# Two sparse-attention stages: VectorE divides both halves of a unit one behind the other, then masks both halves of the next unit

## The chip, the cores and the metric

The kernel runs on one core of a Trainium2 chip. The metric is the device time of one execution in microseconds (us), less is better. All operands are 32-bit floats; the large products are split into high and low parts by the kernel itself.

## What is computed

The reference is three transformer layers over 512 tokens of width 1024. The first two are an MLA (latent attention) layer and an HGRN2 layer, each with an MLP. The third mixes three branches of one input: a sparse attention with an index (DSA, 16 heads of 64, top 128 keys), a native sparse attention (NSA, 16 heads in 2 groups, with a compressed, a selected and a window part) and a state-space branch. The change touches the parts of DSA and NSA that are plain masked attention over 512 keys:

```python
# DSA, per block of 128 queries
s = jnp.einsum('bqhd,bqkd->bqhk', qb, k_sel).astype(jnp.float32) * scale
s = jnp.where((sel <= t[None, :, None])[:, :, None, :], s, NEG)
p = jax.nn.softmax(s, axis=-1).astype(v.dtype)
return jnp.einsum('bqhk,bqkd->bqhd', p, v_sel)
# NSA adds its parts, each times a gate
return gb[..., 0:1] * o_cmp + gb[..., 1:2] * o_slc + gb[..., 2:3] * o_win
```

The kernel does not gather the selected keys. It takes the scores of all keys up to the query's block and adds a mask that holds minus 1e30 where a key is not selected.

## The kernel before

The program is one stream of instructions for each engine, and the engines meet through semaphores alone. Its stages follow each other: MLA, MLP, HGRN, MLP, DSA, NSA, state space, output, MLP. The projections between are dense matmuls of TensorE (lines 385 to 387).

`Pairs` (line 1933) is the helper of the two stages that the change touches. A pair is two heads, one on partitions 0 to 63 and one on 64 to 127 of the same tile; these are its two halves. DSA has 8 pairs and one kind of key, so 8 units. NSA has 8 pairs and two kinds (selected keys and window keys, with their own masks), so 16 units. A unit n is worked in this way, and each step has a name that the text uses:

- **scores** (TensorE, line 2011): 16 matmuls of both halves, key times query, into PSUM banks that all units share. It waits until both halves of unit n-1 are masked, since it overwrites their scores.
- **mask** (VectorE, lines 2118 to 2129), one half: a copy of the query factors (2118), a zeroed sum (2121), four fused operations that scale the scores, add the mask and take the row's maximum (2124, of 128 x 128, 256, 384 and 512), and the maximum times minus one (2129). It waits for the scores of the unit.
- **exp** (ScalarE, line 2076), one half: four activations that also sum their rows. It waits for the mask of that half.
- **divide** (VectorE, lines 2136 to 2144), one half: one over the sum (2136), in NSA times the gate (2139), and four products that scale the probabilities (2144). It waits for the exp of that half.
- **turn** (TensorE, line 2028), one half: ten transposes in three pieces, into two PSUM banks in turn. The third piece waits until the first has been copied out.
- **keep** (ScalarE, line 2083), one half: three copies of the turned pieces out of PSUM.
- **out** (TensorE, line 2047): 16 matmuls of both halves, value times probabilities. In NSA, at each pair's first kind, 8 small products of the compressed part go in front (line 2690).
- **finish** (ScalarE, line 2090): the copy of a pair's result out of PSUM; each unit has one in DSA, every second in NSA.

GpSimd copies the pair's queries into place (line 1973). Every engine has a written order of its own, a `body` per turn of the loop. For one unit n they are, before the change:

- TensorE: turn(n, 0), out(n-1), turn(n, 1), scores(n+2)
- ScalarE: keep(n, 0), exp(n+1, 0), keep(n, 1), finish(n-1), exp(n+1, 1)
- VectorE: divide(n, 0), mask(n+1, 0), divide(n, 1), mask(n+1, 1)

The body of VectorE is the part that changes:

```python
for n in range(per):
    for half in range(2):
        divide(i, n, half)
        if n + 1 < per or nxt:
            mask(i, n + 1, half)
```

`per` is the number of units in a turn, 4 in both stages. DSA has two turns, both written out. NSA has four, the middle two in a loop of the engine. `nxt` is false only in the last turn, so that the last unit has divides and no masks.

Of the kernel before, what the change touches and what calls it, by code (L numbers as in the profile page):

```python
# [1932 lines left out]
class Pairs:  # L1933
# [178 lines left out]
    def dve(self, dve, M, gate=None):  # L2112
        A, V, per = self.name, self.view, len(self.items)

        def mask(i, n, half):
            u, kind = self.item(n)
            m, x = self.kinds[kind][2](half), 2 * (n % 2) + half
            dve.tensor_copy(V.inv[:, x, :], self.factors(M, i, u + n // per * self.unroll, half))
            dve.drain()
            dve.wait_ge(M.sem(f"{A}_scores"), i * per + (n + 1))  # L2120
            dve.memset(V.sum[:, x, :], 0.0)
            for t in range(QT):
                at = PAIR_S_AT[half][t]
                dve.tensor_tensor_reduce(V.p[x][:, CAUSAL_AT[t]:CAUSAL_AT[t] + S_LEN[t]], M.ps[:, at:at + S_LEN[t]],  # L2124
                                         m[:, CAUSAL_AT[t]:CAUSAL_AT[t] + S_LEN[t]],
                                         V.inv[:, x, t:t + 1], -3.0e38,
                                         ALU.add, ALU.max, V.top[:, x, t:t + 1])
            dve.drain()
            dve.tensor_scalar(V.ntop[:, x, :], V.top[:, x, :], -1.0, None, ALU.mult)\  # L2129
               .then_inc(M.sem(f"{A}_masked"), 1)  # L2130

        def divide(i, n, half):
            u, kind = self.item(n)
            x = 2 * (n % 2) + half
            dve.wait_ge(M.sem(f"{A}_exp"), i * (2 * per) + (2 * n + half + 1))
            dve.reciprocal(V.inv[:, x, :], V.sum[:, x, :])
            dve.drain()
            if gate:
                dve.tensor_tensor(V.inv[:, x, :], V.inv[:, x, :], gate(i, u + n // per * self.unroll, half, kind),
                                  ALU.mult)  # L2140
                dve.drain()
            for t in range(QT):
                s = V.p[x][:, CAUSAL_AT[t]:CAUSAL_AT[t] + S_LEN[t]]
                d = dve.tensor_scalar(s, s, V.inv[:, x, t:t + 1], None, ALU.mult)  # L2144
            d.then_inc(M.sem(f"{A}_probs"), 1)

        def body(i, nxt):
            for n in range(per):
                for half in range(2):
                    divide(i, n, half)  # L2150
                    if n + 1 < per or nxt:
                        mask(i, n + 1, half)

        mask(0, 0, 0)
        mask(0, 0, 1)
        self.loop(dve, body)


# [1698 lines left out]
```

## Time and profile before

| | us |
|---|---|
| median of 3 runs | 2777.93 |
| lowest, highest | 2777.47, 2778.92 |
| the profiled execution, its own time | 2784.97 |
| its span in the trace | 2783.2 |
| DSA's units, scores(0) to the next stage's first matmul | 1398.79 to 1486.27 |
| NSA's units, the same | 1652.35 to 1812.26 |

TensorE is busy for 95% of the span, VectorE for 59%, ScalarE for 41%. In the two stages named all three are busy for most of the time. A busy share is read with its stretch; the order in which the engines release each other is read from the timeline, where each row has a start, a duration, the engine, the line, the tiles written and read, and in brackets how long the engine was idle before it and what ended that. "issue" there means that the profile shows no releaser.

### The profile page before, as it was taken

What the parts mean: (1) busy time and instruction counts of PE and PEld (TensorE: products, weight loads), DVE (VectorE), ACT (ScalarE), POOL (GpSimd) and SP (SyncE); (2) the same over time, 40 slices, a digit from 0 to 9 for tenths busy, and PEclk for the clock granted to TensorE, in tenths of its full rate; (3) what the DMA queues carried; (4) which work ended last, traced back from release to release, by engine and by line L of the source; (5) the groups of instructions that cost most, each with busy time, mean ns of one, the idle gap of its engine ahead of it and who ended that gap; (6) DMA issues with size and microseconds to landing.
All of it is one profiled execution on the core that took longest, in us unless ns stands there. A gap on an engine that the chain in (4) does not pass through costs nothing.

```text
span 2783.2 us, 38256 instructions
## 1 busy us (share of the span) xinstructions
PE 2647.9 (95%) x13607; PEld 2122.7 (76%) x13607; DVE 1639.7 (59%) x3082; ACT 1146.7 (41%) x1990; POOL 121.6 (4%) x106
## 2 busy tenths in 40 slices
PE   7999999999999999999989989899999989999998
PEld 5567888888887788888856865577777768788887
DVE  6235725547876843637874278756677675473452
ACT  4444322226674322225474338722455562322221
POOL 0000000000000000001310010000111110000000
PEclk9999999999999999999999999999999999999999
DMA  4112332321222233323201210022222213323231
GB/s 144 46 47 75 100 105 91 98 91 61 82 77 80 72 106 94 102 84 99 76 24 47 98 39 1 16 76 83 76 69 69 74 48 103 132 91 98 91 104 62
DMA packets 59683, 217.80 MB, mean 78 GB/s; under 512 B 6432, under 2 KB 6560, under 8 KB 59424
## 3 DMA queue, kind: packets, MB, share of 16 engines
q1 hardware_dynamic: 57920, 209.76, 23.9%
q0 software_dynamic: 1632, 6.29, 0.7%
q8 instruction: 82, 1.34, 0.2%
q14 instruction: 49, 0.40, 0.0%
HBM read 211.83 MB, written 4.19 MB: 78 GB/s over the span
## 4 chain that ended last, share of the span: by engine, by line
PE 75%; DVE 14%; DVEq 4%; issue 3%; ACT 3%; ACTq 0%; DMA 0%; POOL 0%; SPq 0%
PE ps L385 22%; PE ps L386 21%; PE ps L387 21%; DVE work L2124 2%; PE ps L526 1%; DVE ring_lo L325 1%; DVE big L3362 1%; DVEq L3420 1%; DVE big L2124 1%; PE ps L777 1%; DVE work L2144 1%; DVE work L2476 1%; DVEq L2479 1%; ACT ring_hi L318 1%; PE ps L587 1%
## 5 line engine op out<-in xcount | busy, mean ns | idle before, releaser
L385 PE MATMUL ps<-a_hi,ring_hi 128*128 128x512 f32 (+1 forms) x1896 | 750.6, 396 | 32.7 <-DVE ring_lo L325 19.0
L387 PE MATMUL ps<-a_hi,ring_lo 128*128 128x512 f32 (+1 forms) x1912 | 741.9, 388 | 0.0
L325 DVE TENSOR_TENSOR ring_lo<-ring,ring_hi 128x1024 fp32r<-128x1024 f32 x356 | 435.4, 1225 | 482.1 <-ACT ring_hi L318 451.4
L386 PE MATMUL ps<-a_lo,ring_hi 128*128 128x512 f32 (+1 forms) x1832 | 712.1, 389 | 0.0
L318 ACT ACTIVATE ring_hi<-ring 128x1024 fp32r<-128x1024 f32 x376 | 395.5, 1055 | 502.9 <-PE ps L387 502.8
L385 PEld LDWEIGHTS ps<-a_hi,ring_hi 128*128 128x128 f32 x1896 | 358.6, 189 | 119.3 <-DVE ring_lo L325 17.9
L387 PEld LDWEIGHTS ps<-a_hi,ring_lo 128*128 128x128 f32 x1912 | 361.8, 189 | 74.4
L386 PEld LDWEIGHTS ps<-a_lo,ring_hi 128*128 128x128 f32 x1832 | 346.4, 189 | 68.4 <-issue 1.0
L386 PE MATMUL ps<-hid_lo,ring_hi 128*128 128x512 f32 (+1 forms) x992 | 380.0, 383 | 0.0
L385 PE MATMUL ps<-hid_hi,ring_hi 128*128 128x512 f32 (+1 forms) x928 | 354.8, 382 | 0.0
L387 PE MATMUL ps<-hid_hi,ring_lo 128*128 128x512 f32 (+1 forms) x928 | 354.4, 382 | 0.0
L386 PEld LDWEIGHTS ps<-hid_lo,ring_hi 128*128 128x128 f32 x992 | 187.0, 189 | 36.0
L1326 ACT ACTIVATE sq<-ps 128x512 f32<-128x512 f32 x96 | 57.4, 598 | 350.1 <-PE ps L387 297.9
L385 PEld LDWEIGHTS ps<-hid_hi,ring_hi 128*128 128x128 f32 x928 | 174.5, 188 | 33.9
L387 PEld LDWEIGHTS ps<-hid_hi,ring_lo 128*128 128x128 f32 x928 | 174.5, 188 | 33.5
L1344 DVE TENSOR_TENSOR ssum<-sq,ps 128x512 f32<-128x512 f32 x96 | 65.9, 686 | 87.7 <-ACT sq L1326 81.8
L2011 PE MATMUL ps<-big,work 64*128 64x256 f32 (+3 forms) x384 | 66.0, 487 | 15.2 <-DVE work L2129 13.0
L2076 ACT ACTIVATE work<-work 128x128 f32<-128x128 f32 (+3 forms) x128 | 70.1, 551 | 11.1 <-DVE work L2129 10.1
L2124 DVE CUSTOM_DVE_ANT_0 work<-ps,work 128x128 f32<-128x128 f32 (+3 forms) x128 | 62.8, 547 | 19.2 <-issue 19.2
L2011 PEld LDWEIGHTS ps<-big,work 64*128 64x128 f32 x384 | 47.4, 207 | 34.8 <-issue 19.4
L1065 DVE TENSOR_TENSOR hid_lo<-ssum,hid_hi 128x512 f32 (+1 forms) x96 | 66.4, 692 | 12.4 <-issue 1.1
L1346 DVE TENSOR_TENSOR ssum<-ssum 128x512 f32<-128x512 f32 x96 | 66.5, 692 | 7.2
(456 smaller groups left out, 3304.1 us busy)
## 6 DMA issues: line engine op xcount, KB each, us to landing
ring<-weights SPq DMA_DIRECT2D x392, 512.0 KB, 3.5
h<-x SPq DMA_DIRECT2D x1, 2048.0 KB, 9.2
residual<-h POOLq DMA_DIRECT2D x4, 512.0 KB, 3.5
h<-residual POOLq DMA_DIRECT2D x1, 2048.0 KB, 11.0
out<-h POOLq DMA_DIRECT2D x1, 2048.0 KB, 7.9
tab<-tables SPq DMA_DIRECT2D x1, 1648.0 KB, 15.4
big<-positions SPq DMA_DIRECT2D x1, 256.0 KB, 3.3
col<-columns SPq DMA_DIRECT2D x1, 164.5 KB, 3.9
```

What stands on the lines that cost most here:

```text
L318: act.activation(hi, M.ring[:, b % RING, :], ACT.Copy).then_inc(M.sem("blocks_rounded"), 1)
L325: dve.tensor_tensor(lo, M.ring[:, b % RING, :], hi.bitcast(F32), ALU.subtract).then_inc(M.sem("blocks_split"), 1)
L385: pe.matmul(out, w_hi, hi, start=start, stop=False)
L386: pe.matmul(out, w_hi, lo, start=False, stop=False)
L387: return pe.matmul(out, w_lo, hi, start=False, stop=stop)
L1065: dve.tensor_tensor(lo, src, hi.bitcast(F32), ALU.subtract)
L1326: act.activation(M.sq[:, u % 2, :], M.bank(u % 4), ACT.Relu).then_inc(free, 1)
L1344: dve.tensor_tensor(M.ssum[:, :], M.sq[:, u % 2, :], M.norm_bank(norm), ALU.mult)
L1346: dve.tensor_tensor(M.ssum[:, :], M.ssum[:, :], M.ssum[:, :], ALU.mult)
L2011: mm = pe.matmul(M.ps[:, at:at + S_LEN[t]], self.staged[rows, u, t * P:(t + 1) * P], self.kinds[kind][0][rows, 0:S_LEN[t]], start=True, st ...
L2076: e = act.activation(s, s, ACT.Exp, bias=V.ntop[:, x, t:t + 1], scale=1.0, accum_out=V.sum[:, x, t:t + 1])
L2124: dve.tensor_tensor_reduce(V.p[x][:, CAUSAL_AT[t]:CAUSAL_AT[t] + S_LEN[t]], M.ps[:, at:at + S_LEN[t]], m[:, CAUSAL_AT[t]:CAUSAL_AT[t] + S_ ...
```

## The change

Only the order of VectorE's steps inside `Pairs.dve` changes. For each unit both divides come first, then both masks of the next unit: divide(n, 0), divide(n, 1), mask(n+1, 0), mask(n+1, 1). The operations, their operands, their semaphores and the counts waited for are the same, and the other engines' orders are the same.

```diff
@@ -2148,7 +2148,8 @@
             for n in range(per):
                 for half in range(2):
                     divide(i, n, half)
-                    if n + 1 < per or nxt:
+                if n + 1 < per or nxt:
+                    for half in range(2):
                         mask(i, n + 1, half)
 
         mask(0, 0, 0)
```

VectorE, in DSA, from the divide of one half to the divide that follows. Line 2136 opens a divide, line 2118 a mask. Before:

```order
L2136 RECIPROCAL work<-work 128x4
L2144 TENSOR_SCALAR work<-work 128x128
L2144 TENSOR_SCALAR work<-work 128x256
L2144 TENSOR_SCALAR work<-work 128x384
L2144 TENSOR_SCALAR work<-work 128x512
L2118 COPY work<-inv 128x4
L2121 MEMSET work 128x4
L2124 ISA work<-ps,work 128x128
```

After the change, at the same place:

```order
L2136 RECIPROCAL work<-work 128x4
L2144 TENSOR_SCALAR work<-work 128x128
L2144 TENSOR_SCALAR work<-work 128x256
L2144 TENSOR_SCALAR work<-work 128x384
L2144 TENSOR_SCALAR work<-work 128x512
L2136 RECIPROCAL work<-work 128x4
L2144 TENSOR_SCALAR work<-work 128x128
L2144 TENSOR_SCALAR work<-work 128x256
L2144 TENSOR_SCALAR work<-work 128x384
L2144 TENSOR_SCALAR work<-work 128x512
L2118 COPY work<-inv 128x4
L2121 MEMSET work 128x4
```

The second divide has moved ahead of the first mask; the first mask now stands behind the wait of the second divide.

ScalarE, in DSA, the same before and after the change, one unit: keep of half 0 (line 2083), exp of half 0 of the next unit (2076), keep of half 1, finish (2090), exp of half 1.

```order
L2083 ACTIVATE big<-ps 128x512 x2
L2083 ACTIVATE big<-ps 128x256
L2076 ACTIVATE work<-work 128x128
L2076 ACTIVATE work<-work 128x256
L2076 ACTIVATE work<-work 128x384
L2076 ACTIVATE work<-work 128x512
L2083 ACTIVATE big<-ps 128x512 x2
L2083 ACTIVATE work<-ps 128x256
L2090 ACTIVATE big<-ps 128x512
L2076 ACTIVATE work<-work 128x128
L2076 ACTIVATE work<-work 128x256
```

Nothing moved here. The exp of half 1 stands behind the keep of half 1 and the finish.

## Rows read from the trace of the kernel before

**Rows 1.** The page: span, and busy time of each engine.
```profile
span 2783.2 us, 38256 instructions
...
PE 2647.9 (95%) x13607; PEld 2122.7 (76%) x13607; DVE 1639.7 (59%) x3082; ACT 1146.7 (41%) x1990; POOL 121.6 (4%) x106
```

**Rows 2.** Busy by stretch: PE, PEld, DVE, ACT, POOL (count), clock; DSA, NSA.
```profile
1423.45:1467.03 43.58, 38.68 (x261) 24.91 (x262) 35.93 (x161) 39.20 (x115) 1.23 (x2) 0.99 0.00 1
1674.23:1792.20 117.97, 105.79 (x790) 69.51 (x791) 98.48 (x444) 99.02 (x292) 6.25 (x17) 1.00 0.00 1
```

**Rows 3.** Timeline of one DSA unit, all engines: start, us, engine, line, tiles.
```profile
1449.59 0.34 DVE L2124 CUSTOM_DVE_ANT_0 work<-ps,work 128x128 f32<-128x128 f32 x1 [1.11 <-issue]
...
1451.64 0.17 DVE L2129 TENSOR_SCALAR work<-work 128x4 f32<-128x4 f32 x1
1451.72 0.17 DVE L2136 RECIPROCAL work<-work 128x4 f32<-128x4 f32 x1
...
1451.85 0.40 ACT L2076 ACTIVATE work<-work 128x128 f32<-128x128 f32 x1
...
1453.34 0.71 ACT L2076 ACTIVATE work<-work 128x512 f32<-128x512 f32 x1
...
1453.46 0.35 DVE L2124 CUSTOM_DVE_ANT_0 work<-ps,work 128x128 f32<-128x128 f32 x1
...
1454.24 1.51 ACT L2083 ACTIVATE big<-ps 128x512 f32<-128x512 f32 x3
...
1455.51 0.17 DVE L2129 TENSOR_SCALAR work<-work 128x4 f32<-128x4 f32 x1
...
1455.65 0.59 ACT L2090 ACTIVATE big<-ps 128x512 f32<-128x512 f32 x1
...
1455.83 2.43 PE L2011 MATMUL ps<-big,work 64*128 64x256 f32 x16 [0.50 <-DVE work L2129]
1455.84 1.27 DVE L2144 TENSOR_SCALAR work<-work 128x128 f32<-128x128 f32 x4
1456.12 0.40 ACT L2076 ACTIVATE work<-work 128x128 f32<-128x128 f32 x1
...
1458.21 0.19 ACT L2076 ACTIVATION_READ_ACCUMULATOR work<-work 128x1 f32 x1
1458.31 0.34 DVE L2124 CUSTOM_DVE_ANT_0 work<-ps,work 128x128 f32<-128x128 f32 x1 [1.12 <-issue]
```

**Rows 4.** DSA's second scores, and the first mask of its third unit.
```profile
1407.85 4.63 PE L2011 MATMUL ps<-big,work 64*128 64x256 f32 x16 [3.83 <-DVE work L2129]
...
1423.45 0.34 DVE L2124 CUSTOM_DVE_ANT_0 work<-ps,work 128x128 f32<-128x128 f32 x1 [3.32 <-issue]
```

**Rows 5.** The last DSA unit: its first mask, a gap of TensorE, its last divide.
```profile
1467.03 0.34 DVE L2124 CUSTOM_DVE_ANT_0 work<-ps,work 128x128 f32<-128x128 f32 x1 [1.11 <-issue]
...
1474.95 1.58 PE L2028 MATMUL ps<-tab,work 128*128 128x128 f32 x8 [2.18 <-DVE work L2144]
1475.03 0.71 ACT L2076 ACTIVATE work<-work 128x512 f32<-128x512 f32 x1
1475.87 0.18 DVE L2136 RECIPROCAL work<-work 128x4 f32<-128x4 f32 x1 [0.97 <-ACT work L2076]
```

**Rows 6.** VectorE in NSA: third unit's first mask, one divide, last unit's first mask.
```profile
1674.23 0.34 DVE L2124 CUSTOM_DVE_ANT_0 work<-ps,work 128x128 f32<-128x128 f32 x1 [2.44 <-issue]
...
1730.70 0.17 DVE L2136 RECIPROCAL work<-work 128x4 f32<-128x4 f32 x1
...
1732.80 0.35 DVE L2124 CUSTOM_DVE_ANT_0 work<-ps,work 128x128 f32<-128x128 f32 x1
...
1792.11 0.34 DVE L2124 CUSTOM_DVE_ANT_0 big<-ps,tab,work 128x128 f32<-128x128 f32 x1 [0.96 <-issue]
```

**Rows 7.** Busy by stretch (columns of rows 2) around the gap before 1474.95.
```profile
1471.00:1474.00 3.00, 1.51 (x12) 1.04 (x10) 2.60 (x12) 2.85 (x9) 0.00 (x0) 1.00 0.01 3
1475.00:1478.50 3.50, 3.33 (x14) 1.95 (x16) 1.45 (x5) 2.33 (x7) 0.00 (x0) 0.56 0.01 2
```

## The prediction

> **What bounds the kernel now.** I read the page first, for the size of the thing [rows 1]: TensorE is busy for 95% of a span of 2783.2 us, nearly all of it in dense matmuls that the change does not touch. The two stages that it does touch have 7 and 15 steps from one unit to the next. So I read the busy time by stretch there [rows 2]. From the first mask of DSA's third unit to that of its eighth there are 5 periods in 43.58 us, 8.72 each, and no engine fills them: TensorE 38.68, ScalarE 39.20, VectorE 35.93. In NSA, from the third unit to the sixteenth, there are 13 periods in 117.88 us [rows 6], 9.07 each, again with all three engines between 83% and 90% busy [rows 2]. Neither stage is bound by one engine; a ring of waits through several sets the period, and the timeline shows which.
>
> In a DSA unit [rows 3] VectorE starts the first mask at 1449.59, when the scores are there, and ends it at 1451.81 (1451.64 + 0.17). The divide of half 1 starts at 1451.72, the second mask runs from 1453.46 to 1455.68, and only then may TensorE begin the next scores, 1455.83, which let the next first mask start at 1458.31. That is the ring: mask, divide, mask, scores, 8.72 us. The other divide lies under the scores and leaves VectorE 1.12 us of idle time. Read ScalarE beside it: exp of half 0 starts at 1451.85, keep of half 1 at 1454.24, finish at 1455.65, exp of half 1 at 1456.12, to 1458.40. That exp ends 1.3 us after the divide of half 0 (1455.84 + 1.27 = 1457.11). Nobody minds now, because a mask comes before the divide that needs it.
>
> **The change, part by part.** No operation is added or removed, so the busy times stay. Only VectorE's order moves, and three edges with it.
>
> Gain: one divide leaves the ring of scores. The two masks now stand together, so the next scores can start earlier. The most that this frees is the divide with its hand-over, 1453.46 - 1451.72 = 1.74 us a unit.
>
> Cost: the divide of half 1 now stands in front of the next unit's first mask and waits for the exp of half 1. Queued behind it are both masks, and behind these the next scores and both next exps. Follow the new ring from one exp of half 0 to the next, with durations of rows 3:
>
> - exp 0 itself, 1451.85 to 1454.05 (1453.34 + 0.71): 2.20
> - keep of half 1, 1454.24 to 1455.65: 1.41
> - finish, 1455.65 to 1456.12: 0.47
> - exp 1, 1456.12 to 1458.40 (1458.21 + 0.19): 2.28
> - from there to the divide: 0.04, by the one place where VectorE waits for such an exp now, DSA's last unit, 1475.87 after 1475.83 (1475.03 + 0.71 is 1475.74, and the sum's read ends 0.09 behind it as in rows 3) [rows 3, 5]
> - the divide of half 1 up to the next mask, 1451.72 to 1453.46: 1.74
> - the first mask up to exp 0, 1449.59 to 1451.85: 2.26
>
> Sum 10.40 us, against 8.72: ScalarE's keep and finish, which stood beside the masks, now stand in the ring. 5 periods cost 5 x 10.40 - 43.58 = +8.4.
>
> In NSA the divide with its gate takes 2.10 up to the next mask [rows 6], so the sum is 10.76, and 10.29 in units without a finish. Of the 13 periods 6 have one: 6 x 10.76 + 7 x 10.29 = 136.6, less 0.7 since the first and last turns are written out and their gated divide is about 0.1 shorter, against 117.88: +18.0.
>
> The edges. The first two periods of DSA are set by scores at the low clock (4.63 us [rows 4]) and the first mask of unit 2 is at 1423.45. In the new order masks come earlier there, exp 0 of unit 1 starts at the same time as now, and the same durations, counted on from there without a finish, put the first mask of unit 2 at about 1423.0 (an estimate): -0.4. In the last unit there is no mask behind the divides; from its first mask to its last divide it takes 8.84 now [rows 5] and 2.26 + 2.20 + 1.41 + 0.47 + 2.28 + 0.04 = 8.66 after, and the keeps behind start some 0.5 earlier: -0.5. NSA the same, -0.2 and -0.5. Together -1.6.
>
> The clock. TensorE has 7.74 us of work in a DSA unit and 8.14 in an NSA unit (38.68 / 5, 105.79 / 13 [rows 2]) and will get 10.4, so it stands still for some 2.5 us, nearly all of it at one place: after two pieces of turn 1 it waits for keep of half 1, which waits for exp 0. Now a gap of 2.18 us [rows 5] is followed by transposes that take 1.58 for 8, and the granted clock goes from 1.00 to 0.56 over the next 3.5 us [rows 7], that is to the lower level (1.2 GHz) for most of them. Scores at that level take 4.63 instead of 2.43 [rows 3, 4]. They would start about 3.2 us after exp 0 (its 2.20, one 128 x 512 copy of 0.59 as in finish, two transposes at 0.2) and end about 7.8 after it; the next mask can start at 10.40 - 2.26 = 8.14, so even they are covered. What could show is what follows them: turn 0, out and turn 1 each start later, by up to 0.3 us in DSA, and by about 1.3 in an NSA unit whose out has the compressed products in front. The nearest bounds are 0 (always covered) and 5 x 0.3 + 6 x 1.3 = 9.3. I take +4, near the middle, since the gap is longer than the one that cost the clock, but not every gap can.
>
> Sum: 8.4 + 18.0 - 1.6 + 4 = **+28.8 us**. The profiled execution has 2784.97 in its own time (1.8 more than its span) and stands 7.0 above the median of the runs; the difference is put on the median: 2777.93 + 28.8 = 2806.7, **2807**.
>
> **The rivals.**
>
> *A, faster: the divides hide the scores.* Mechanism: with the masks together the scores start 1.74 earlier in the ring, the two divides fill the time that they take, and VectorE's 1.12 us of idle time before each first mask goes. The period would fall to what the busiest engine needs, 39.20 / 5 = 7.84 in DSA and 105.79 / 13 = 8.14 in NSA [rows 2]: -0.88 x 5 - 0.93 x 13 = -16.5, 2761. It decides at one place: exp 1 must be done when divide 0 is. Rows 3 have it 1.3 us late even now, and it would have to come earlier still. The Trainium skill, Perfetto Trace Analysis, section Identifying the Most-Contended Engine, says that the engine with the highest occupancy is the one to improve, and that one closes its gaps by making what it waits for start sooner. By that rule this change helps, since it moves the scores and so TensorE's work ahead; the rows above say that an engine at 90% with a fixed order can be in the ring without being the bound.
>
> *B, no change: ScalarE is free in time.* If keep and finish were done when the second mask ends, the ring would be exp 1, divide, mask, mask: 0.04 + 2.28 + 0.04 + 1.74 + 2.22 + 0.22 + 2.22 = 8.76, in NSA 9.12, so 5 x 0.04 + 13 x 0.05 = +1, 2779. For it: the turn of half 1 can start a mask earlier than now. Against it: exp 0 takes ScalarE first, by its written order, and keep and finish need 1.88 behind it, so exp 1 starts 4.08 after exp 0 whatever TensorE does, and the second mask ends at 2.44.
>
> *C, much slower: the low clock enters the ring.* If the gap brings the clock down in every unit and out and turn 1 run at it too, the 2.2 us of the scores can no longer be covered: up to 18 x 2.2 = 40 more, 2847. Against it: by rows 7 the low clock does not last for a whole period of 10.4, and a delayed TensorE has no gap, so the next unit is at full clock.
>
> *D: the order is not what the source says.* The instructions as issued show the divides together in both stages, so I give it nothing.
>
> **How the numbers follow.** My forecast 0.84, A 0.05, B 0.06, C 0.05. All are told apart by a measurement, whose bound is about 0.2% or 5.6 us: the forecast and C are slower, A faster, B the same. The predicted time is the forecast's, 2807. Its own range: at the low end the clock costs nothing and a hand-over or two overlap better than I let them (0.3 us in each of 18 periods, 5), 2777.93 + 24.8 - 5 = 2798; at the high end the clock costs the whole 9.3 and each period another 0.3, 2777.93 + 24.8 + 9.3 + 5.4 = 2817. I stretch that a little to 2796 to 2820. A and B stay outside below with 0.11 and C above.
>
> **What would show it.** Right: the time from one first mask to the next is about 10.4 in DSA, and in NSA 10.3 and 10.8 by turns; VectorE's idle time stands before line 2136, released by ScalarE's line 2076, one wait a unit of about 2.5 us, and no longer before line 2124; ScalarE goes from exp 0 through keep and finish to exp 1 with no idle time; the scores end before the divide does; TensorE waits some 2.5 us for keep in a unit, with patches of low clock. Wrong: a wait before line 2124 on scores in most units (C), ScalarE idle before exp 1 with the mask ending last (B), or periods under 8.7 (A). A change outside 1403 to 1486 and 1655 to 1812 would be none of mine.

## The result, and the profile after

| | before | after |
|---|---|---|
| median, us | 2778.43 | 2809.55 |
| lowest to highest, 4 runs each | 2777.47 to 2780.84 | 2807.75 to 2811.0 |
| the profiled execution, its own time | 2784.97 | 2809.23 |

The ratio is 1.0104, with a 95% interval of 1.0088 to 1.012. The changed kernel is slower by 31.1 us (24.5 to 33.3).

The page of the changed kernel has the same counts of instructions and nearly the same busy times as [rows 1]; TensorE differs by 0.3 us.

```profile
span 2807.4 us, 38256 instructions
...
PE 2647.6 (94%) x13607; PEld 2120.8 (76%) x13607; DVE 1644.1 (59%) x3082; ACT 1143.9 (41%) x1990; POOL 121.9 (4%) x106
```

Busy by stretch of the changed kernel, with the columns of [rows 2]: from the first mask of the third unit to that of the last, DSA and NSA.

```profile
1420.17:1472.73 52.56, 41.30 (x264) 26.44 (x262) 36.69 (x161) 38.87 (x116) 0.62 (x1) 0.94 0.00 1
1678.75:1816.44 137.69, 112.51 (x798) 73.78 (x798) 101.05 (x444) 98.72 (x295) 6.29 (x17) 0.95 0.00 1
```

The work per stretch is what it was, and the stretches are longer: 52.56 us for 43.58 in DSA, 137.69 for 117.88 in NSA. VectorE and ScalarE are busy for about as long (36.69 for 35.93, 38.87 for 39.20 in DSA). TensorE is busy for longer, 41.30 for 38.68 in DSA, with a granted clock of 0.94 where it was 0.99. The first masks stand at 1420.17, 1430.55, 1441.53, 1451.98, 1462.36 and 1472.73, so the periods are 10.38, 10.98, 10.45, 10.38 and 10.37, for 8.71 or 8.72 before. In NSA they run by turns, from the third unit on: 10.60, 10.99, 10.35, 10.88, 10.32, 10.90, 10.35, 10.82, 10.32, 10.80, 10.38, 10.84, 10.14.

The timeline of one DSA unit of the changed kernel, with the columns of [rows 3]:

```profile
1451.98 0.35 DVE L2124 CUSTOM_DVE_ANT_0 work<-ps,work 128x128 f32<-128x128 f32 x1
...
1454.24 0.40 ACT L2076 ACTIVATE work<-work 128x128 f32<-128x128 f32 x1 [2.56 <-DVE work L2129]
...
1456.43 1.49 ACT L2083 ACTIVATE big<-ps 128x512 f32<-128x512 f32 x3
...
1456.56 0.18 DVE L2136 RECIPROCAL work<-work 128x4 f32<-128x4 f32 x1
...
1457.06 0.44 PE L2028 MATMUL ps<-tab,work 128*128 128x128 f32 x2 [2.48 <-ACT big L2083]
1457.43 2.43 PE L2011 MATMUL ps<-big,work 64*128 64x256 f32 x16
1457.82 0.59 ACT L2090 ACTIVATE big<-ps 128x512 f32<-128x512 f32 x1
1458.29 0.40 ACT L2076 ACTIVATE work<-work 128x128 f32<-128x128 f32 x1
...
1460.61 0.18 DVE L2136 RECIPROCAL work<-work 128x4 f32<-128x4 f32 x1 [2.51 <-ACT work L2076]
...
1462.36 0.35 DVE L2124 CUSTOM_DVE_ANT_0 work<-ps,work 128x128 f32<-128x128 f32 x1
```

Read it against [rows 3]. VectorE's wait of 1.11 or 1.12 us in front of the first mask is gone: the mask at 1462.36 follows the divides, and the scores it needs ended at 1459.86, 2.5 us before. In its place stands a wait of 2.51 us at 1460.61, in front of the divide of half 1, released by ScalarE. ScalarE itself waits 2.56 us for the first mask and then works through from 1454.24 to 1460.57. And TensorE has a gap of 2.48 us in front of the third piece of turn 1.

The chain of waits of the changed kernel over the same unit (start, us, what):

```profile
1454.24 2.29 ACT work L2076 x8
1456.53 0.49 ACT big L2083
1457.02 0.04 issue
1457.06 0.45 PE ps L2028 x2
1457.54 0.39 ACT big L2083
1457.92 0.48 ACT big L2090
1458.41 2.17 ACT work L2076 x8
...
1460.61 0.18 DVE work L2136
```

Exp 0, keep of half 1, finish, exp 1, divide: the chain runs through ScalarE, with a step over TensorE inside keep (its third copy waits for the two transposes), and the scores are not in it.

The waits of the changed kernel over DSA (engine, line, waited for; us in total, times, longest) put them in numbers. Before the change the row `DVE work L2124 <- issue` stood at 12.2 us in 8 waits of DSA; it has gone down to the two waits of the stage's start, and a row for line 2136 has come.

```profile
DVE work L2136 <- ACT work L2076: 17.7, 8, 2.8
...
DVE work L2124 <- issue: 1.2, 2, 0.9
```

**Where the 31 us are.** DSA's units take 96.21 us (1396.36 to 1492.57), 8.73 more than before; NSA's take 179.64 (1656.64 to 1836.28), 19.72 more. Together 28.45. The rest of the two profiled executions differs by 4.2 us the other way: the part ahead of DSA is 2.43 shorter, the part between the stages 2.0, the part behind 0.2 longer. The change touches none of it, and the profiled execution of before stood 7 us above its median. Of the 31.1 us between the medians 2.7 are thus found in no row, and they lie inside the interval of the measurement. The ends of a stage vary by as much without any change: from NSA's first scores to its third first mask it is 21.88 us in the kernel before and 19.16 in `dsa_only` (below), where NSA has the same code. What the periods show is firmer than what the edges show.

### The profile page after: what moved, and what is told of

Its sections match the earlier page's. It is cut to its first block, busy times and chain, and to the rows that moved or that the text cites. A ratio compares the mean times of both kernels' runs of the same rounds, so it can differ in the third digit from the quotient of the medians.

```text
span 2807.4 us, 38256 instructions
## 1 busy us (share of the span) xinstructions
PE 2647.6 (94%) x13607; PEld 2120.8 (76%) x13607; DVE 1644.1 (59%) x3082; ACT 1143.9 (41%) x1990; POOL 121.9 (4%) x106
## 4 chain that ended last, share of the span: by engine, by line
PE 74%; DVE 12%; ACT 7%; DVEq 4%; issue 2%; ACTq 0%; DMA 0%; POOL 0%; SPq 0%
PE ps L385 22%; PE ps L387 21%; PE ps L386 21%; ACT work L2076 2%; PE ps L526 1%; DVE ring_lo L325 1%; DVE big L3363 1%; ACT big L2076 1%; DVE work L2124 1%; DVEq L3421 1%; PE ps L777 1%; DVE work L2477 1%; DVEq L2480 1%; ACT ring_hi L318 1%; PE ps L587 1%
## 5 line engine op out<-in xcount | busy, mean ns | idle before, releaser
L2028 PE MATMUL ps<-tab,work 128*128 128x128 f32 x320 | 52.0, 296 | 37.4 <-ACT big L2083 34.0
L2028 PEld LDWEIGHTS ps<-tab,work 128*128 128x128 f32 x320 | 36.0, 147 | 53.6 <-ACT big L2083 39.7
```

The source lines that it names most:

```text
L2028: mm = pe.transpose(M.ps[:, at:at + P], s, M.t("ident", P))
```

## Experiments

Ten kernels. The theory is the prediction's ring: with the divides together, exp 0, keep of half 1, finish, exp 1, divide and mask follow each other, 10.4 us. The rivals change with each experiment. All times are against the kernel before on the same chip, whose medians there were 2779.15, 2780.29 and 2778.72. A period is the time from one first mask to the next.

### One stage at a time

`dsa_only` has the new order in DSA alone, `nsa_only` in NSA alone (the diff is from the changed kernel; the other has `!= "nsa"` and `== "nsa"`).

```diff
                     divide(i, n, half)
-                if n + 1 < per or nxt:
+                    if A != "dsa" and (n + 1 < per or nxt):
+                        mask(i, n + 1, half)
+                if A == "dsa" and (n + 1 < per or nxt):
                     for half in range(2):
                         mask(i, n + 1, half)
```

> The new order in DSA alone, NSA as before. Theory (ring: exp 0, keep, finish, exp 1, divide, mask, 10.4 us a period where 8.7 stood): the extra belongs to each stage by its number of periods, so DSA alone gives what its stage shows in the trace, 96.21 - 87.48 = +8.7 us, ratio 1.0031. Rival (something outside the two stages, or one of them alone, carries most of the +31): under +3 or over +15.

Measured: 2786.1, ratio 1.0022 (1.0012 to 1.0033), +7. DSA's periods go to 10.37 and 10.38, with one of 10.73, and NSA's 13 take 117.94 together, as before (117.88).

> The new order in NSA alone, DSA as before. Theory: the stage's own 179.64 - 159.92 = +19.7 us, ratio 1.0071; together with the run on DSA alone that is 28.4 of the 31. Rival (the two stages add to something larger through the clock or the weights that are loaded between): the two runs together miss 31 by more than 5.

Measured: 2800.54, ratio 1.0072 (1.0048 to 1.0097), +20 to +21. NSA's 13 periods take 137.74, DSA's five 43.58.

So the periods of each stage change with its own order and not with that of the other. 7 and 20.5 make 27.5, near the 28.45 that the two traces show and within the interval of the whole.

### Is finish in the ring?

`finish_last` lets ScalarE do finish behind exp 1. VectorE keeps the new order.

```diff
                 keep(i, n, 1)
-                if n or not isinstance(i, int) or i:
-                    finish(i, n - 1)
                 if n + 1 < per or nxt:
                     exp(i, n + 1, 1)
+                if n or not isinstance(i, int) or i:
+                    finish(i, n - 1)
```

> The changed kernel with one step of ScalarE moved: finish stands behind exp of half 1, not in front of it. Theory: finish is 0.47 us of the ring in 6 periods of DSA and 6 or 7 of NSA, so these periods fall to about 9.9 and 10.3, and the time by about 5.5 us, to +25.5 over before. Rival 1 (the period is set by TensorE at the low clock, or by scores): no change, +31. Rival 2 (the ring is mask, exp 1, divide, mask and ScalarE is late only by chance): far more than 0.47 comes back.

Measured: 2805.73, ratio 1.0097 (1.0081 to 1.0114), +26.6. DSA's quiet periods fall to 9.90, which is 0.47 less to the hundredth: the 0.47 that the prediction gave finish. In NSA the total falls by 0.5 alone (137.18 for 137.69). The six periods with a finish add up to 63.09 for 65.23, which is 0.36 less in each where the term is 0.47; the seven others add up to 74.09 for 72.46, and one of them takes 11.61, from the first mask at 1717.72 to that at 1729.33. The timeline of `finish_last` around it:

```profile
1712.22 0.69 PE L2028 MATMUL ps<-tab,work 128*128 128x128 f32 x2 [2.57 <-ACT big L2083]
1712.84 4.64 PE L2011 MATMUL ps<-big,work 64*128 64x256 f32 x16
...
1717.41 1.53 PE L2028 MATMUL ps<-tab,big 128*128 128x128 f32 x8
...
1719.56 1.09 PE L2691 MATMUL ps<-work 128*64 128x128 f32 x16
...
1722.74 1.09 PE L2028 MATMUL ps<-tab,big 128*128 128x128 f32 x8
1723.43 1.09 ACT L2083 ACTIVATE work<-ps 128x512 f32<-128x512 f32 x2 [1.17 <-PE ps L2028]
```

The scores take 4.64 instead of 2.43, turn 0 starts late behind them, the compressed products and the out follow, and turn 1 comes at 1722.74, so late that keep, which stands in the ring, waits 1.17 us for it. So the term is right in DSA and somewhat smaller in NSA, and a late TensorE can take back what it saves, in the units whose out has the compressed products in front.

### ScalarE's keep out of the way of exp 1

`exps_together` lets ScalarE do both exps one behind the other, then keep of half 1 and finish. If keep and finish between the exps were the whole trouble, this would mend it.

```diff
                     exp(i, n + 1, 0)
+                if n + 1 < per or nxt:
+                    exp(i, n + 1, 1)
                 keep(i, n, 1)
                 if n or not isinstance(i, int) or i:
                     finish(i, n - 1)
-                if n + 1 < per or nxt:
-                    exp(i, n + 1, 1)
```

> The changed kernel with ScalarE in the order keep 0, exp 0, exp 1, keep 1, finish. Rival (ScalarE's order alone is the cause, and freeing exp 1 heals it): the ring is exp 1, divide, mask, mask, 8.76 us, and the time falls to +1 to +3 over before. Theory: it does not heal, since TensorE's order then closes a second ring of the same length: the third piece of turn 1 waits for keep 1, which now waits for exp 1, and the next scores stand behind that piece: mask to mask end 4.66, exp 1 2.24, first copy 0.64, two transposes 0.4, scores 2.47, sum 10.4 us for every period. So about +30, and VectorE's idle time moves from line 2137, released by ScalarE, to the first line 2125, released by scores.

Measured: 2822.47, ratio 1.0151 (1.0127 to 1.0175), +43. It mends nothing: another ring of the same length takes over. The third piece of turn 1 waits for a copy of keep, keep now stands behind exp 1, and TensorE has the scores behind that piece. A quiet and a disturbed unit of `exps_together`, in its timeline:

```profile
1440.37 0.44 PE L2028 MATMUL ps<-tab,work 128*128 128x128 f32 x2 [2.01 <-ACT big L2083]
1440.74 4.09 PE L2011 MATMUL ps<-big,work 64*128 64x256 f32 x16
...
1444.89 0.34 DVE L2124 CUSTOM_DVE_ANT_0 work<-ps,work 128x128 f32<-128x128 f32 x1 [3.41 <-issue]
...
1462.76 0.44 PE L2028 MATMUL ps<-tab,work 128*128 128x128 f32 x2 [2.47 <-ACT big L2083]
1463.13 2.43 PE L2011 MATMUL ps<-big,work 64*128 64x256 f32 x16
...
1465.62 0.34 DVE L2124 CUSTOM_DVE_ANT_0 work<-ps,work 128x128 f32<-128x128 f32 x1 [1.75 <-issue]
```

In the quiet unit the period is the 10.4 expected (1455.25 to 1465.62 is 10.37). In the disturbed one the scores take 4.09 instead of 2.43, and since the next mask waits for them the period grows by as much, to 12.03. Its busy time by stretch, over three periods of 11.45, 12.03 and 10.36, then over two of 10.36 and 10.37:

```profile
1421.41:1455.25 33.84, 26.04 (x157) 16.88 (x158) 21.96 (x96) 23.45 (x69) 1.23 (x2) 0.90 0.00 1
1455.25:1475.98 20.73, 15.18 (x105) 9.73 (x106) 14.59 (x64) 15.76 (x46) 0.00 (x0) 1.00 0.00 0
```

The expected +30 missed by 13, and the suspect is the clock: 0.90 in the stretch with the long periods, 1.00 in the other.

### Is it the clock?

To show that, TensorE's gap was filled with products whose result nobody reads, ahead of the third piece of turn 1. Nothing else changes against `exps_together`. The first attempt, `exps_together_filled`, put 8 of them behind the wait for keep (the cut shows these lines alone).

```diff
+                if half and piece == 2 and fill:
+                    pe.wait_ge(M.sem(f"{A}_masked"), i * (2 * per) + 2 * (n + 2))
+                    idle_pe(pe, M, 0, 8)
                 for k in tiles:
```

> The kernel with the exps together, and 8 matmuls of 128 x 256 (about 0.24 us each at the high clock) whose result nobody reads, in TensorE's gap of 2.48 us before the third piece of turn 1. They write a score bank after both masks of the unit have read it and before the next scores overwrite it. Theory: that kernel is at +43 and not at +30 since its gap brings TensorE's clock down and its scores stand in the ring, where the low clock costs 1 to 2.6 us a period (11.5 to 13.0 seen where 10.37 stands in quiet periods). With the gap filled all periods are 10.4 to 10.5, and the time is about +30 over before. Rival (the long periods are of something else, such as the order of the keeps): no better than +43, or worse by the filler's own 1.9 us a unit where it is late.

Measured: 2889.76, ratio 1.0387 (1.0371 to 1.0403), +109: a badly made kernel. The filler stands behind the wait and not in it, and each product shows as two matmuls:

```profile
1466.46 5.41 PE L482 MATMUL ps<-tab 128*128 128x256 f32 x16 [2.46 <-ACT big L2086]
```

The gap stays at 2.46 us and 5.41 us are added to a ring that has the scores in it; DSA's periods of 15.2 to 15.6 are about 10.4 + 5. It tells nothing of the clock. `exps_together_filled2` has half as many, ahead of the wait for keep.

```diff
+                if half and piece == 2 and fill:
+                    pe.wait_ge(M.sem(f"{A}_masked"), i * (2 * per) + 2 * (n + 2))
+                    idle_pe(pe, M, 0, 4)
                 if c >= 2 or not isinstance(i, int) or i:
```

> The same as the kernel filled first, mended in two ways: the filler stands in front of TensorE's wait for the copied piece, not behind it, and it is 4 products, which the trace of the first shows as 8 matmuls of 0.24 us, 1.9 us in all, where the gap is 2.48. Theory: TensorE is then never idle for long, its scores take 2.43 us in each period, and all periods of DSA are 10.4 and of NSA 10.4 to 10.6, so about +30 over before where the kernel without filler has +43. Rival (the long periods have another cause): +43 or more.

Measured: 2808.14, ratio 1.0101 (1.0083 to 1.0119), +29.4. Its timeline shows the gap cut to 0.74 us. From DSA's third scores on all take 2.43 us, in both stages, but one in NSA that takes 2.59:

```profile
1438.04 0.44 PE L2031 MATMUL ps<-tab,work 128*128 128x128 f32 x2 [0.74 <-ACT big L2086]
1438.41 2.43 PE L2011 MATMUL ps<-big,work 64*128 64x256 f32 x16
```

Busy by stretch of `exps_together`, 110 us of NSA:

```profile
1690.00:1800.00 110.00, 86.73 (x575) 56.66 (x571) 76.04 (x326) 73.92 (x220) 5.79 (x15) 0.91 0.00 1
```

And of `exps_together_filled2`, the same stretch:

```profile
1690.00:1800.00 110.00, 102.57 (x716) 70.41 (x715) 83.82 (x364) 80.71 (x239) 6.25 (x17) 1.00 0.00 1
```

More work, less time: the clock goes from 0.91 to 1.00 here (in 60 us of DSA from 0.94 to 0.99), DSA's periods are 10.35 to 10.37 throughout, and 14 of the 43 us are gone. That is what the lower level (1.2 GHz) cost in `exps_together`. The slow scores say the same: ten of the 24 there take 3.5 to 4.6 us in place of 2.43 from the third on, 14.7 us more in all. Of the 29.4 that stay, 26.3 lie in the 18 periods (51.81 for 43.58, 135.93 for 117.88), which are the ring's.

### Other ways to give the new order room

Two kernels keep VectorE's new order, and change the orders of the other two engines so that neither ring forms. `exps_and_scores` has both exps together and also puts the scores ahead of turn 1 on TensorE. Mask of half 1 writes a buffer that turn 1 of two units before reads; the place of the scores had covered that, so the mask gets a wait for it. ScalarE's edit is that of `exps_together` and is left out of the cut.

```diff
                     out(i, n - 1)
-                turn(i, n, 1)
                 if n + 2 < per or nxt:
                     scores(i, n + 2)
+                turn(i, n, 1)
...
             dve.wait_ge(M.sem(f"{A}_scores"), i * per + (n + 1))
+            if half and (n > 1 or not isinstance(i, int) or i):
+                dve.wait_ge(M.sem(f"{A}_turned"), i * (6 * per) + 6 * (n - 1))
```

> The changed kernel with both orders mended: ScalarE does keep 0, exp 0, exp 1, keep 1, finish, and TensorE does turn 0, out, scores, turn 1. The mask of half 1 gets a wait for the turn of the unit two before, whose probabilities it overwrites and which the old order of TensorE had covered. Theory: keep and finish are then in no ring; what is left is exp 1, divide, mask, mask: 8.76 us in DSA and 9.12 in NSA, so the time is +1 to +4 over before, same within what can be measured. Rival (the period is bound by something the two order edits don't touch, the clock or the amount of VectorE's work): it stays above +15.

Measured: 2782.6, ratio 1.0005 (0.9996 to 1.0015), +1 to +2; the interval holds no change. DSA's quiet periods are 8.84. `keeps_first` copies before it works: ScalarE keep 0, keep 1, exp 0, exp 1, finish, and TensorE turn 0, turn 1, out, scores.

```diff
                 turn(i, n, 0)
+                turn(i, n, 1)
                 if n or not isinstance(i, int) or i:
                     out(i, n - 1)
-                turn(i, n, 1)
...
                 keep(i, n, 0)
+                keep(i, n, 1)
                 if n + 1 < per or nxt:
                     exp(i, n + 1, 0)
-                keep(i, n, 1)
+                    exp(i, n + 1, 1)
                 if n or not isinstance(i, int) or i:
                     finish(i, n - 1)
-                if n + 1 < per or nxt:
-                    exp(i, n + 1, 1)
```

> The changed kernel with ScalarE in the order keep 0, keep 1, exp 0, exp 1, finish and TensorE in the order turn 0, turn 1, out, scores. Another way to take keep and finish out of the ring, which uses that both divides are done early. No new wait is needed. Theory: again the ring exp 1, divide, mask, mask, 8.76 and 9.12 us, +1 to +4 over before; in NSA's units whose out has the compressed products the scores are 1 us later and may show. Rival (the divides of a unit side by side are bad in themselves): above +15.

Measured: 2782.28, ratio 1.0011 (1.0001 to 1.002), +2 to +3. DSA's quiet periods are 8.76 to 8.78. In both the loss of 31 is all but gone with VectorE's order of the change kept. So that order is not slow in itself; it is slow with ScalarE's and TensorE's orders as they stood. And it is no gain either: what binds DSA now is the ring that rival B named (exp 1, divide, mask, mask), 8.76 by the prediction's sum. For NSA that is not shown: its periods are mostly 9.2 to 9.4 in both kernels where 9.12 was expected (the 13 take 121.79 and 121.45), and what holds them up was not followed. VectorE still waits in the ring, in DSA of `exps_and_scores`:

```profile
1444.78 0.18 DVE L2138 RECIPROCAL work<-work 128x4 f32<-128x4 f32 x1 [0.80 <-ACT work L2076]
```

### A version that beats both

In that ring one divide stands between exp 1 and the masks. `divide_last` has, beside the edits of `exps_and_scores`, VectorE's order divide 0, mask 0, mask 1, divide 1. Now the divide of half 1 stands in front of no mask that its own wait could hold back.

```diff
-                for half in range(2):
-                    divide(i, n, half)
+                divide(i, n, 0)
                 if n + 1 < per or nxt:
-                    for half in range(2):
-                        mask(i, n + 1, half)
+                    mask(i, n + 1, 0)
+                    mask(i, n + 1, 1)
+                divide(i, n, 1)
```

> A version that may beat both. VectorE: divide 0, mask 0, mask 1 of the next unit, divide 1, so that no mask stands behind the divide that waits for exp 1. ScalarE: keep 0, exp 0, exp 1, keep 1, finish. TensorE: turn 0, out, scores, turn 1. The mask of half 1 waits for the turn of the unit two before. Theory: the ring of before loses the divide (mask, mask, scores: 2.44 + 2.22 + 0.15 + 2.47 = 7.3), so the period is set by work and hand-overs of the engines, 8.1 to 8.5 us against 8.72 and 9.07: -4 to -12 us, most likely -7, against before. Rival 1: the turns of half 1 are late and keep stands in a new ring, period 9 or more, no gain. Rival 2: TensorE's clock falls in the gaps and the scores stand in the ring: slower than before by up to 20.

Measured: 2771.92 (2768.48 to 2773.12), ratio 0.9966 (0.9952 to 0.9979), so 8 to 9 us below the kernel before (6 to 13) and some 38 below the changed one. DSA's quiet periods are 8.33 or 8.34. In its timeline, one unit:

```profile
1434.82 0.34 DVE L2126 CUSTOM_DVE_ANT_0 work<-ps,work 128x128 f32<-128x128 f32 x1 [0.48 <-issue]
...
1439.45 0.17 DVE L2138 RECIPROCAL work<-work 128x4 f32<-128x4 f32 x1
...
1440.67 2.43 PE L2011 MATMUL ps<-big,work 64*128 64x256 f32 x16
...
1441.06 0.18 DVE L2138 RECIPROCAL work<-work 128x4 f32<-128x4 f32 x1
...
1443.16 0.34 DVE L2126 CUSTOM_DVE_ANT_0 work<-ps,work 128x128 f32<-128x128 f32 x1 [0.49 <-issue]
```

Neither divide waits. VectorE's only wait in a unit is 0.49 us for the scores, where it was 1.12 in [rows 3]. In 40 us of DSA (1425 to 1465) TensorE is busy for 36.49, VectorE for 34.60 and ScalarE for 37.03.

The periods carry less of the gain than was expected of them. DSA's five take 41.97 for 43.58, and NSA's 13 take 115.70 for 117.88: they run from 8.31 to 9.84, 8.90 on average, where 8.1 to 8.5 was expected. That is 3.8 us together. Another 3.2 lie at DSA's start, from its first scores to its third first mask: 21.45, where three executions with the old order of VectorE there (before, `nsa_only` and `old_order_freed`, below) have 24.66 or 24.67. The rest is at NSA's two ends. Its start takes 19.15 for 21.88, and since `dsa_only` has 19.16 there with the old code, that part is not shown to be a gain of the order.

Is the gain VectorE's order or the freed orders of the others? `old_order_freed` has ScalarE's and TensorE's orders and the wait of `divide_last`, and VectorE's order of the kernel before (the cut is against `exps_and_scores`).

```diff
                     divide(i, n, half)
-                if n + 1 < per or nxt:
-                    for half in range(2):
+                    if n + 1 < per or nxt:
                         mask(i, n + 1, half)
```

> VectorE's order as before the change (divide 0, mask 0, divide 1, mask 1), with the other engines as in the version that beats before (exps together, scores in front of turn 1, and the wait of the mask of half 1). Theory: the ring of before is untouched by that, mask, divide, mask, scores, 8.72 and 9.07, so the time is that of before, 0 to +5; it takes VectorE's order as well to gain. Rival (the gain came from the two edits on ScalarE and TensorE, whatever VectorE does): -5 to -8.

Measured: 2784.94, ratio 1.0021 (1.001 to 1.0032), +6, one more than the top of what was expected. DSA's periods are 8.78 and 8.79, NSA's 13 take 119.11. So freeing the others gains nothing alone: the gain needs VectorE's order too. Whether that order gains with the other two as they stood before was not run. Why NSA is 1.2 us longer here than before was not followed up.

## Why the prediction was right

2807 stood against 2809.55 measured, +28.8 against +31.1, and the traces hold +28.45. Step by step:

- **What bounds the kernel.** Right: rings and no single engine. The Trainium skill, Perfetto Trace Analysis, section Identifying the Most-Contended Engine, says to improve the engine with the highest occupancy first (how its gaps are closed stands in the section behind it, Optimization Strategy). The prediction read that as a case for moving TensorE's scores ahead. But in DSA the busiest engine was ScalarE (39.20 of 43.58), not TensorE (38.68), and after the change both have a smaller share (38.87 and 41.30 of 52.56). In NSA TensorE was the busiest, and fell from 105.79 of 117.97 to 112.51 of 137.69. So the trace does not refute the rule, since the change did not close that engine's gaps. It shows that the occupancies do not tell which order of the waits sets the period.
- **The ring of DSA, 10.40.** Right. Quiet periods are 10.37 and 10.38, and its steps follow each other in the chain of waits. By the timeline they start thus: exp 0 at 1454.24, keep 1456.43, finish 1457.82, exp 1 1458.29, divide 1460.61, mask 1462.36, which is 2.19, 1.39, 0.47, 2.32 and 1.75, for 2.20, 1.41, 0.47, 2.28 + 0.04 and 1.74; with the 2.26 from the first mask (1451.98) to exp 0 it makes 10.38. `finish_last` confirms the 0.47 in DSA by itself.
- **NSA, 10.76 and 10.29.** Right. The periods run 10.8 to 11.0 with a finish and 10.1 to 10.6 without, and the 13 take 137.69, for 135.9 (136.6 less 0.7) without the clock.
- **The edges, -1.6.** Mis-sized: they are -0.25 in DSA and -0.09 in NSA (8.73 less the 8.98 of the five periods, 19.72 less the 19.81 of the thirteen). DSA's first units gained 0.85, for 0.4 forecast. In its tail the 0.5 forecast is there: from the last first mask to the last divide it takes 8.63 for 8.84, and the out behind comes another 0.33 earlier. But that out runs at the low clock, 4.22 us where the kernel before has 3.10, and so the tail takes 0.6 more:

```profile
1482.48 4.22 PE L2047 MATMUL ps<-big 128*64 128x512 f32 x16
```

  NSA's start took 0.2 more for 0.2 less forecast, and its tail 0.3 less for 0.5 less. With 2.7 us between two executions of the same code at NSA's start, nothing is to be read from these.
- **The clock, +4.** Over-sized: what the periods hold beyond the ring is 0.6 in DSA (52.56 less 5 x 10.40) and 1.8 in NSA (137.69 less 135.9), 2.4 in all, and not all of it is the clock's. One unit of DSA met the low level (granted clock 0.50 from 1436.0 to 1441.5), the one with the period of 10.98:

```profile
1435.62 0.69 PE L2028 MATMUL ps<-tab,work 128*128 128x128 f32 x2 [2.48 <-ACT big L2083]
1436.24 4.64 PE L2011 MATMUL ps<-big,work 64*128 64x256 f32 x16
...
1436.35 0.38 ACT L2083 ACTIVATE big<-ps 128x256 f32<-128x256 f32 x1 [0.30 <-PE ps L2028]
...
1439.42 0.18 DVE L2136 RECIPROCAL work<-work 128x4 f32<-128x4 f32 x1 [2.76 <-ACT work L2076]
...
1440.87 0.16 DVE L2118 COPY work<-inv 128x4 f32<-128x4 f32 x1
...
1441.48 0.06 DVE L2121 MEMSET work<- 128x4 f32 x1 [0.46 <-issue]
```

  Two things add to 0.6 there, and one of them is the clock's. The two transposes ahead of the scores, which are in the ring, take 0.69 for 0.44, keep waits 0.30 for them, and the divide comes 0.24 later after its first mask than in the quiet unit (8.87 for 8.63). The other is VectorE's stop of 0.46 in front of the memset, which puts the mask 2.11 after that divide for 1.75. The memset is where VectorE waits for the scores, but these end at 1440.88 (1436.24 + 4.64), before the copy in front of it ends (1441.03). And `dsa_only` has the same stop in its one long period, 10.73, behind scores at full speed that ended 2.8 us before:

```profile
1437.91 2.43 PE L2011 MATMUL ps<-big,work 64*128 64x256 f32 x16
...
1442.53 0.17 DVE L2118 COPY work<-inv 128x4 f32<-128x4 f32 x1
...
1443.15 0.06 DVE L2121 MEMSET work<- 128x4 f32 x1 [0.46 <-issue]
```

  So the slow scores themselves cost nothing: the prediction had them covered with 0.3 to spare, and covered they were. In NSA scores of 3.85, 4.12 and 3.74 us (at 1748.24, 1769.40 and 1790.77) stand in periods of 10.35, 10.32 and 10.38, as long as those with 2.43. What the rows give to the clock is 0.24 in this unit, at most 0.07 in the one behind it (10.45 for 10.38) and 1.1 in the out of DSA's tail. How much of NSA's 1.8 is the clock's was not taken apart. The delay that the prediction did forecast, of turn 1 behind the out in NSA, is the one that `finish_last` shows at 1722.74.
- The two errors, 1.3 too little for the edges and 1.6 too much for what the periods hold beyond the ring, nearly cancel (-1.6 + 4 against -0.3 + 2.4). The sum of the traces, 28.45, is nearer to 28.8 than its terms deserve, and that is luck. The 26.4 of the two rings, the bulk of the forecast, is not.
- **Rival A** (faster) needed exp 1 done when divide 0 is. It is 2.5 us late by the wait at 1460.61; it was 1.3 late before. **Rival B** (8.76) needed ScalarE free of keep and finish in time, which the changed kernel does not give; `keeps_first` gives it, and has its 8.76 to 8.78 in DSA. **Rival C** (the low clock in the ring) did not happen in the changed kernel; `exps_together` brings the scores into the ring and pays 14 us for it, not the 40 of the bound. **D** did not apply.

What stays open: the 2.7 us between the medians and the traces, why one period of DSA met the low clock and its neighbours with the same gap did not, and what stops VectorE for 0.46 us in front of a memset now and then. The kernel before has such a stop too, at 1714.76, with nothing waited for that was not there.

## What to carry to other kernels

An engine with a written order is a queue: a step moved ahead of others puts its own wait in front of all of them, and whatever the engine it waits for does first is then in the ring. Before reordering one engine, write down every ring through it as a sum of durations from one unit of the timeline, with the orders of the other engines in it; the longest gives the period, and where two are near each other, one engine's order gains nothing until the others' are changed with it (here 0.34% faster with three orders changed together; with parts of them 1.04% and 0.21% slower, or the same within the interval). And see which step of TensorE lies in the ring before counting the cost of its idle gaps.

## What the runs showed of the hardware

- Gaps of TensorE of 2.0 to 2.6 us were enough for its clock to fall in many units, and not in all. In `exps_together` the scores behind a gap of 2.01 us took 4.09, and behind one of 2.47 they took 2.43. With the gap cut to 0.74 us in DSA all the scores behind such gaps took 2.43.
- The price depends on where the slow work stands. In the changed kernel the scores of one unit took 4.64 us instead of 2.43 and did not delay the next mask; what showed of the low clock in that period was 0.24 us, from the two slow transposes that are in the ring. With the scores in the ring (`exps_together`) the slow units made up some 14 us of the whole time.
- A product of 32-bit floats shows as two matmul rows: 8 fillers were 16 rows and took 5.41 us, 0.34 a row behind a gap of 2.46. It is so with the scores and the out as well: their 16 in the text and the rows are 8 products in the source. The ten transposes of a turn are ten rows.
- VectorE can stop for 0.46 us in front of an instruction whose semaphore is already up (`dsa_only` at 1443.15, 2.8 us after the scores had ended).
